# Slots of the split weight ring 1028 words apart in place of 1024

## The reference, cut to what matters

```python
# first block
h = rmsnorm(x, norm_mix_g);  proj = h @ w_in              # 1024 x 5632
...                                                       # recurrence, convolution, gates
x = x + merged @ w_out
x = x + peer_ffn(rmsnorm(x, norm_ffn_g), ...)             # 16384 single-neuron experts, U and V 16384 x 1024
# second block, two layers
for layer in range(2):
    x = x + 0.5 * swiglu(rmsnorm_2(x, ...), gate, up, down)   # width 2816
    x = x + mixer(...)                                        # attention and pooling, or block attention
    x = x + 0.5 * swiglu(rmsnorm_2(x, ...), gate, up, down)
return rmsnorm_2(x, norm_final)
```

## Time and profile before

| | |
|---|---|
| median of 3 runs | 2041.37 us (2040.89 to 2041.47) |
| span of the profiled execution | 2039.6 us |
| own time of the profiled execution | not listed apart from its span; the runs' median is 1.8 us above the span |
| PE busy, matmuls | 2005.6 us (98%), x13232 |
| PEld busy | 1822.9 us (89%) |
| DVE busy | 1508.3 us (74%) |
| ACT busy | 1123.1 us (55%) |
| granted clock of TensorE | 0.998 of full speed |
| DMA | 353.73 MB, mean 173 GB/s |

### The profile page before, as it was taken

One profiled execution on the slowest core, in us unless ns is written; L12 is line 12 of the kernel. 1 busy time (PEld: TensorE's weight loads), 2 busy tenths in 40 slices (PEclk: granted clock), 3 DMA queues, 4 the chain that ended last, 5 costly groups with the idle time before them and its releaser, 6 DMA issues.

```text
span 2039.6 us, 37233 instructions
## 1 busy us (share of the span) xinstructions
PE 2005.6 (98%) x13232; PEld 1822.9 (89%) x13232; DVE 1508.3 (74%) x2564; ACT 1123.1 (55%) x1835; POOL 59.9 (3%) x40
## 2 busy tenths in 40 slices
PE   7999999999999999999999999999999999999998
PEld 6999999988888888888888999999999999999998
DVE  5868898877777777777777667776667667957666
ACT  5445537965555555555555555755555555655554
POOL 0000430000000000000000000000000000000000
PEclk9999999999999999999999999999999999999999
DMA  6445543055565666655665555455555555445553
GB/s 214 135 135 190 205 142 104 24 174 187 189 192 192 187 189 192 191 189 187 206 231 173 187 186 174 135 169 188 187 186 178 185 185 186 156 143 177 185 188 111
DMA packets 101466, 353.73 MB, mean 173 GB/s; under 512 B 11392, under 2 KB 16640, under 8 KB 101120
## 3 DMA queue, kind: packets, MB, share of 16 engines
q1 hardware_dynamic: 100944, 350.13, 52.5%
q10 hardware_dynamic: 432, 2.36, 0.3%
HBM read 348.77 MB, written 3.67 MB: 173 GB/s over the span
## 4 chain that ended last, share of the span: by engine, by line
PE 90%; DVE 7%; ACT 2%; issue 1%; DMA 0%; SPq 0%; DVEq 0%; ACTq 0%
PE front L2030 38%; PE acc L2030 35%; PE tile L2030 16%; DVE w_lo L1219 2%; ACT w_hi L715 1%; DVE rstd L1241 1%; ACT h_parts L741 0%; DMA raw<-stream 0%; PE front L2587 0%; DVE cand L1688 0%; DVE h_parts L1248 0%; DVE sq L1230 0%; DVE conv L1573 0%; DVE rest L1657 0%; DVE top_i L1653 0%
## 5 line engine op out<-in xcount | busy, mean ns | idle before, releaser
L1219 DVE TENSOR_TENSOR w_lo<-raw,w_hi 128x1024 fp32r<-128x1024 f32 x612 | 747.0, 1223 | 85.4 <-ACT w_hi L715 84.9
L715 ACT CAST w_hi<-raw 128x1024 fp32r<-128x1024 f32 x628 | 654.3, 1044 | 137.6 <-PE tile L2030 60.8
L2030 PE MATMUL front<-h_parts,w_hi 128*128 128x512 f32 (+1 forms) x2432 | 586.4, 377 | 4.2 <-ACT h_parts L741 2.5
L2030 PEld LDWEIGHTS front<-h_parts,w_hi 128*128 128x128 f32 x2432 | 436.5, 189 | 80.2 <-issue 2.4
L2030 PE MATMUL front<-h_parts,w_lo 128*128 128x256 f32 x2272 | 337.2, 282 | 0.0
L2030 PEld LDWEIGHTS front<-h_parts,w_lo 128*128 128x128 f32 x2272 | 318.8, 190 | 20.6
L2030 PE MATMUL tile<-h_parts,w_hi 128*128 128x256 f32 x1344 | 247.8, 286 | 5.1 <-DVE w_lo L1219 2.6
L2030 PEld LDWEIGHTS tile<-h_parts,w_hi 128*128 128x128 f32 x1344 | 209.5, 192 | 8.2 <-issue 4.9
L1304 DVE TENSOR_TENSOR scaled<-front,scaled 128x512 f32<-128x512 f32 x76 | 52.6, 692 | 215.1 <-ACT scaled L779 215.1
L2030 PE MATMUL acc<-w_hi,mid_hi 128*128 128x512 f32 x512 | 200.9, 392 | 2.1 <-DVE mid_lo L1793 1.7
L783 ACT ACTIVATE scaled<-scaled 128x256 f32<-128x256 f32 x188 | 78.6, 418 | 223.4 <-DVE scaled L1307 116.6
(11 more groups left out here) (324 smaller groups left out, 2519.5 us busy)
## 6 DMA issues: line engine op xcount, KB each, us to landing
raw<-stream SPq DMA_DIRECT2D x632, 512.0 KB, 3.7
early_u<-stream SPq DMA_DIRECT2D x20, 512.0 KB, 3.6
early_activations<-early_out SPq DMA_DIRECT2D x20, 128.0 KB, 3.5
scaled<-early_activations SPq DMA_DIRECT2D x10, 128.0 KB, 4.0
x<-x_t SPq DMA_DIRECT2D x2, 512.0 KB, 5.3
keysT<-keys_t ACTq DMA_DIRECT2D x1, 1024.0 KB, 6.3
attc<-attention_constants ACTq DMA_DIRECT2D x1, 1024.0 KB, 7.1
out_t<-h SPq DMA_DIRECT2D x4, 256.0 KB, 2.4
```

The lines of the kernel that those rows point to most:

```text
L715: nc.scalar.copy(w_hi[:, s, :], raw[:, s, :]).then_inc(hi_ready, 1)
L1219: nc.vector.tensor_tensor(w_lo[:, s, :], raw[:, s, :], w_hi[:, s, :].bitcast(F32), ALU.subtract).then_inc(lo_ready, 1)
L2030: return nc.tensor.matmul(out, lhsT, rhs, start=start, stop=stop, **kw)
```

## The change

The slots of w_hi and w_lo get a length of D + 4 = 1028 words, of which 1024 are used. Slot 0 begins at a multiple of 64 bytes, slots 1, 2 and 3 begin 16, 32 and 48 bytes past one. w_lo's ring is rounded up to a multiple of 64 words, and so is H_HI, so that slot s of w_lo has the same place within 64 bytes as slot s of w_hi. w_hi stays at word 4096, w_lo moves from 8192 to 8256, and h_parts and all behind it move up by 128 words (512 bytes), which keeps their places within 64 bytes. `raw` is as it was. No instruction is added, removed or moved on any engine; only addresses differ, and the step between two slots in `project_tokens` becomes 1028 words.

```diff
 BASE = 16512
-RAW, W_HI, W_LO = 0, RING * D, 2 * RING * D
-H_HI = 3 * RING * D
+SLOT = D + 4
+RAW, W_HI = 0, RING * D
+W_LO = -(-(W_HI + RING * SLOT) // 64) * 64
+H_HI = -(-(W_LO + RING * SLOT) // 64) * 64
 H_LO = H_HI + KT * T
...
         raw = sb("raw", RAW, [RING, D])
-        w_hi = sb("w_hi", W_HI, [RING, D], F32R)
-        w_lo = sb("w_lo", W_LO, [RING, D], F32R)
+        w_hi = sb("w_hi", W_HI, [RING, SLOT], F32R)[:, :, 0:D]
+        w_lo = sb("w_lo", W_LO, [RING, SLOT], F32R)[:, :, 0:D]
```

## The result

| | before | after |
|---|---|---|
| median of 7 runs each, same chip | 2041.29 us | 2046.87 us |
| range of the runs | 2040.55 to 2041.75 | 2046.14 to 2049.38 |
| span of the profiled execution | 2039.6 | 2044.9 |

The ratio is 1.0032, with a 95% interval of 1.0022 to 1.0041. The kernel is slower by 5.6 us, where I had forecast 9.3 us less. The seven runs of the changed kernel lie in two groups, four from 2046.14 to 2046.87 us at a mean granted clock of 0.998 and three from 2048.76 to 2049.38 at 0.996 to 0.997, and the profile is of one of the first four.

What follows compares the result with a forecast made beforehand. TensorE's matmul pace was taken as the bound; the terms -12.2 + 2.6 + 0.3 summed to -9.3 us, so 2032.1 us against 2041.37. The overall range was 2014 to 2048 us, the forecast's own 2024 to 2038.

Steps and rivals of the forecast that it cites:

- The bound: Whole kernel: the pace of TensorE's matmuls sets the end, with one under way for 2005.6 of 2039.6 us.
- The mechanism: TensorE's two operand reads run side by side; their places within 64 bytes set how often they meet, and so the pace.
- (b): Matmuls of 512 columns, fronts and drains: 2628 displaced at +1 ns, +2.6 us, bounds -8.7 and +13.9 us.
- (a): Matmuls of 256 columns, slab against h_parts or mid: 5544 displaced at 2.2 ns less, -12.2 us, bounds -55 and +29.
- (c): The y stages, 576 matmuls: slot 2 slows by 2.2 ns on 144 of them, +0.3 us, bounds -1 and +2.
- (d): ScalarE's 628 and VectorE's 612 slab splits, writing 16 to 48 bytes later: 0, bounds 0 and +1 us.
- (e): project_tokens' two-slot operand counted elsewhere, loads into raw unchanged, 512-byte shift of the rest harmless: 0.
- The slower one: Rival, chance 0.18: displaced 512-column matmuls never settle at 226.7 ns and stay at 232; 2052 us.
- only slot 2 faster: Part of the slower rival: among displaced 256-column matmuls just slot 2 gains 2.2 ns, giving -3.4 us.
- The large gain: Rival, chance 0.13: both matmul shapes settle 3.3 ns lower in all three displaced slots; 2014.7 us.
- No effect: Rival, chance 0.23: the y stages' pace comes from something else in their address, not place within 64 bytes; 2041.4 us.
- A drain in the others at another steady pace: Sign in the changed profile: drains outside slot 0 change pace; over 231 ns would mean the slower rival is right.

Runs made afterwards that it cites:

- u32: All four slots of w_hi and w_lo begin 32 bytes past alignment, h_parts and mid stay aligned, against the kernel before; 2049.5 us, ratio 1.0040.
- all32: w_hi, w_lo, h_parts, mid and all behind them begin 32 bytes later than in the kernel before; 2041.3 us, ratio 1.0000.
- s64: Slots of w_hi and w_lo spaced by 64 bytes more than in the kernel before; 2039.46 us, ratio 0.999.
- hi256: Only the slots of w_hi spaced by 256 bytes more than in the kernel before; 2041.28 us, ratio 1.0001.
- u48: All four slots of w_hi and w_lo begin 48 bytes past alignment, h_parts and mid stay aligned, against the kernel before; 2049.38 us, ratio 1.0039.
- u16: All four slots of w_hi and w_lo begin 16 bytes past alignment, h_parts and mid stay aligned, against the kernel before; 2043.95 us, ratio 1.0007.
- ffn_mid: Against the kernel before, the dense layers' second product gets its own mid, 32 bytes off, while the drains keep the aligned one; 2037.58 us, ratio 0.9982.
- lo_only: Only w_lo's slots are staggered, 1028 words apart, with w_hi as in the kernel before; 2039.94 us, ratio 0.9994.
- up: Against the kernel before, ring 8 bytes up outside the expert layer, aligned in it; three ScalarE splits wait one slab more; 2029.52 us, ratio 0.9942.

## Why the prediction was wrong

**The bound.** Right. PE's matmuls set the end, VectorE's and ScalarE's busy times stayed within 1.1 us, and the whole difference is in distances between matmuls.

**The mechanism.** Right in its core: the relative place of TensorE's two operands changes the pace (u32 against all32). Two parts of it were wrong, and the second bears on both terms that failed. The period is not 64 bytes: 64, 128 and 192 bytes each have paces of their own (s64), 256 has that of 0 (hi256). And the pace is not a function of the place alone: slot 3 of the changed kernel and slot 3 of u48 have the same addresses and 122.5 against 118.3 ns, slot 3 of the changed kernel has 122.9 and 117.9 in one stage, and u16 has 233 and 226.7 for its long fronts. Rows 4 lie in the last slab of w_in and not in w_out as their heading says; their pace of 120 ns is that of the other tile stages all the same.

**The steps that failed** are the sizes of terms (b) and (a), each for half of the error.

**Term (b), 512 columns.** I took +1 ns for 2628 displaced matmuls, +2.6 us. All long matmuls together cost 9.8 us, which is 3.7 ns for each displaced one; some 1.0 us of it lies on drains in slot 0, which were not displaced and go from 229.0 to 230.6 ns. I had the right row in hand: five long matmuls at 232 ns that then drop to 226.7. I read it as "small loss" although I had named the other end, that they stay there, +13.9 us. They do nearly that where they stay: u48 holds 233 ns in all its long matmuls. The 226.7 is a state, and not of aligned runs alone. In the changed kernel the expert fronts in slot 1, 16 bytes displaced, hold it behind the drain in slot 0 and cost nothing, while those in slot 3 go at 232.3, and the drains in slot 0 reach it only for their last three matmuls. That is why 3.7 and not 5.3 was paid. What brings a displaced run into it, as in the third dense layer of u16, stays open.

**Term (a), 256 columns.** I took -2.2 ns for 5544, -12.2 us. Measured: -4.7 us, 0.85 ns each. I had taken the one price of the y stages for all three slots and all shapes. Three things are in it. The second products were to give 1584 x 2.2 = 3.5 us and gave 0.7, because slot 3 runs slower than aligned (122.5 ns), which takes back what slots 1 and 2 give. The fronts did not start from 120 but from 119.1 to 119.3 ns, since their first ones behind a long run are shorter than 120. And where displaced ones did settle they did so at 118 to 118.4, not at 117.8. The term with its own sign alone would still have made the kernel faster; ffn_mid, where it stands by itself, is faster by 3.4 us.

**Term (c), y.** +0.3 us forecast, +0.6 measured. Right in sign and size, though by an argument whose period was wrong.

**Terms (d) and (e).** 0 and 0; the splits last what they did.

**The sum.** Forecast -12.2 + 2.6 + 0.3 = -9.3; measured -4.7 + 9.8 + 0.6 - 0.6 (all others) = +5.1. Term (b) is 7.2 us of the 14.4 between them, term (a) 7.5, and the others give back 0.3. With (a) as measured and (b) as I took it the sum is -2.1 us, and with (b) as measured and (a) as I took it -2.4, each within what a measurement can tell from no change. Neither error alone turns the sign; the two together do.

**The rivals.** The slower one named what happened to most of the long matmuls. It was to decide from 4.5 ns more per long matmul with term (a) in full; 3.7 came, but term (a) was not in full, and so it decided at less. Its "only slot 2 faster" was wrong in form (in the second products slot 1 is faster too, and slot 3 is slower) and near in effect by luck: -3.4 us against -4.7. Its 2052 lies 5 us above the result. The large gain did not come. No effect is refuted by the trace, and by u32 against all32. The Trainium skill (SBUF — State Buffer, "SBUF: two separate sides") speaks of lines of 16 bytes, by which offsets of 16, 32 and 48 bytes would be alike: here a uniform 16, 32 and 48 gave long expert fronts of 232.9, 233.6 and 232.5 ns where aligned ones have 226.8, so by this case the relation of two operands matters beyond that line. Likewise the Trainium skill (TensorE: Matmul & The Clock Gate, "Step-by-step: what each phase is for") has two independent read ports, so that a weight load takes nothing from the running matmul. The traces don't say what inside TensorE makes the difference; they do say that moving the stationary operand against the moving one changes the pace of the same instructions by up to 7 ns.

**The signs I had named.** "A drain in the others at another steady pace; if that is over 231 ns the slower rival is right" was the useful one: the drain in slot 2 of the changed kernel takes 2.79 us, 232.5 ns each. "If slots 1 and 3 differ from slot 2 in sign, taking one value for the three was wrong" also came true, for slot 3 in the second products. In the tile stages the period came nearly as named: four slabs in a row from 160 us on go at 119.6, 118.4, 118.3 and 117.8 ns in slots 0 to 3.

## What to carry to other kernels

Where TensorE has no idle time, take its pace from start times, for each shape and each buffer slot apart, before touching an address: 120 against 115.6 ns for 256 columns is 4%, and in the durations it shows as 283 against 278 ns, less than half of that share. Place stationary and moving operand by shape: in this kernel runs of 512 columns went best with both at the same place within 256 bytes (u16's third dense layer apart, which went as fast 16 bytes off) and in long runs, and runs of 256 columns with a stationary slab went best with the slab 8 bytes up. Measure each layout in its own program, since paces at one address differed by what surrounds them. When a known row shows a state that settles, the safe price for whatever disturbs it is the unsettled pace and not a part of it; and a buffer that is moved in mid-program changes waits, so look at what else they release.

## What the runs showed of the hardware

- One instruction at one clock (1.00) with one shape has many paces. For 256 columns, slab stationary: 115.6 ns (8 bytes up), 117.4 (8 bytes down), 118.3 (16, 32 or 48 up in all slots), 120.0 (aligned), 122.5 to 122.9 (48 up in slot 3 of the staggered ring, in the second products and in one slab of w_in; 117.9 in another). Slab moving, 256 columns: 119.9 aligned, 116.8 to 116.9 with the ring 32 bytes up, 122.4 to 123.0 with it 8 up. Drains, slab moving in 512 columns: 228.6 with their run-in when aligned, 231.6 to 233.3 at 16 to 48 bytes, 234.0 at 8.
- The aligned long run drops to 226.7 ns after a few matmuls and stays there across the front behind it (226.8 on average in the expert fronts). Displaced runs go at 229 to 234 in most places, but at 226.7 in slot 1 of the changed kernel's expert layer and at 226.6 to 226.8 in the third dense layer of u16.
- Two runs with the same addresses and the same shape can go at different paces, each for all 24 matmuls: 118.3 and 122.5 ns in u48 and the changed kernel, 122.9 and 117.9 within the changed kernel. In lo_only expert fronts whose own operands are not displaced go at 231 ns behind a drain on displaced w_lo and at 226 behind an undisplaced one.
- 3.36 us of idle TensorE, with transposes and another wait behind it, went with a granted clock of 0.50 for some 10 us (1067.1 to 1077.3), which cost 1.95 us in the next twenty matmuls. With idle times of 0.55, 0.39 and 1.73 us in the same place the clock stayed at 1.00.
- Every trace ends at a granted clock of 0.50, and for how long differs: 7.5 us in the kernel before, 7.2 in the changed one, 5.7 in lo_only, 10.7 in s64. Seven of the traces, up among them, also have 3.4 us of it near 33 us. So a difference of 1 to 2 us between two kernels need not come from their paces.
